# Moving averages of the pooled branch on GpSimd, and three changes in the order of ScalarE's small work, in a two-layer hybrid encoder

## The reference, cut to what matters

```python
h = rms_norm(x, norm_w)
proj = jnp.einsum('bld,dn->bln', h, w_in)
(aq, ak, av, ag, bq, bk, bv, bg, cq, ckv, ckr, cg, du, dg) = jnp.split(proj, split_points, axis=-1)
...
q = jnp.einsum('blr,rn->bln', rms_norm(cq_raw, q_lat_w), w_uq)      # branch c: the up-projections
kv = jnp.einsum('blr,rn->bln', rms_norm(ckv_raw, kv_lat_w), w_ukv)
...
# branch d: for group g of 128 channels, window w = 2, 4, 8, 16
mean = (jnp.take(csg, hi, axis=1) - jnp.take(csg, lo, axis=1)) / cnt   # moving mean of u over w tokens
outs.append(mean - u32[..., sl])
...
mixed = jnp.einsum('blgc,gcd->blgd', pooled, w_group).reshape(b, l, BRANCH_W) * scale
...
y = jnp.concatenate([ya * silu(ag), yb * silu(bg), yc * silu(cg), yd * silu(dg)], axis=-1)
return x + jnp.einsum('bln,nd->bld', y, w_out)
```

## Time and profile before

| what | value |
|---|---|
| time, median of 3 runs | 913.06 us (913.02 to 913.20) |
| the profiled execution's own time | 912.77 us |
| its span, first to last instruction | 911.0 us |
| PE, PEld, DVE, ACT, POOL busy | 899.7, 858.4, 637.0, 585.5, 0.2 us |
| granted clock of TensorE, mean | 1.00 |
| HBM read, written | 140.57, 2.10 MB |

### The profile page before, as it was taken

The page is one execution under the profiler, slowest core; times in us unless marked ns, Lnnn a source line. Parts: engine busy times, 40 slices in busy tenths (PEclk is TensorE's granted clock), DMA queues, the critical chain, the costliest instruction groups (busy, mean ns, idle before and its releaser), DMA issues.

```text
span 911.0 us, 18111 instructions
## 1 busy us (share of the span) xinstructions
PE 899.7 (99%) x7054; PEld 858.4 (94%) x7054; DVE 637.0 (70%) x1071; ACT 585.5 (64%) x1045; POOL 0.2 (0%) x4
## 2 busy tenths in 40 slices
PE   8999999999999999999999999999999999999998
PEld 7998998999999999999999989999999999999998
DVE  7785887768777776766665658876687667666552
ACT  7678756678666667745554588566686666675331
POOL 0000000000000000000000000000000000000000
PEclk9999999999999999999999999999999999999999
DMA  8654343343444343445455544334425344445562
GB/s 332 260 188 142 134 142 132 109 139 129 140 141 142 138 148 128 145 149 192 166 195 185 186 155 169 119 119 161 158 93 186 128 151 145 149 171 185 187 201 78
DMA packets 22997, 143.83 MB, mean 158 GB/s; under 512 B 2560, under 2 KB 4736, under 8 KB 6528
## 3 DMA queue, kind: packets, MB, share of 16 engines
q1 hardware_dynamic: 22768, 142.64, 44.0%
q10 hardware_dynamic: 144, 0.04, 0.0%
HBM read 140.57 MB, written 2.10 MB: 157 GB/s over the span
## 4 chain that ended last, share of the span: by engine, by line
PE 89%; ACT 7%; DVE 2%; issue 1%; DMA 1%; SPq 0%; ACTq 0%; DVEq 0%
PE dense L725 25%; PE dense L727 24%; PE dense L726 24%; PE s_ps L889 4%; PE o_ps L924 4%; ACT w_hi L1014 2%; PE norm_ps L845 2%; PE t_ps L905 2%; DVE w_lo L1319 1%; ACT qw L1087 1%; DMA x<-xt_dram 1%; PE swap_ps L860 0%; ACT sq L1084 0%; PE norm_ps L727 0%; PE swap_ps L727 0%
## 5 line engine op out<-in xcount | busy, mean ns | idle before, releaser
L725 PE MATMUL dense<-h_hi,w_hi 128*128 128x272 f32 (+2 forms) x1440 | 427.1, 297 | 1.5 <-DVE h_lo L1299 0.9
L727 PE MATMUL dense<-h_hi,w_lo 128*128 128x272 f32 (+2 forms) x1440 | 412.6, 287 | 0.0
L726 PE MATMUL dense<-h_lo,w_hi 128*128 128x272 f32 (+2 forms) x1440 | 410.6, 285 | 0.0
L1319 DVE TENSOR_TENSOR w_lo<-raw,w_hi 128x1024 fp32r<-128x1024 f32 (+1 forms) x257 | 313.3, 1219 | 88.4 <-ACT w_hi L1014 82.3
L1014 ACT ACTIVATE w_hi<-raw 128x1024 fp32r<-128x1024 f32 (+1 forms) x257 | 271.3, 1056 | 68.7 <-PE dense L727 53.9
L725 PEld LDWEIGHTS dense<-h_hi,w_hi 128*128 128x128 f32 x1440 | 271.3, 188 | 8.2 <-issue 3.8
L726 PEld LDWEIGHTS dense<-h_lo,w_hi 128*128 128x128 f32 x1440 | 271.5, 189 | 1.3
L727 PEld LDWEIGHTS dense<-h_hi,w_lo 128*128 128x128 f32 x1440 | 271.1, 188 | 0.0
L725 PE MATMUL dense<-y_hi,w_hi 128*128 128x272 f32 (+1 forms) x500 | 143.1, 286 | 2.3 <-ACT q_st L1059 1.3
L727 PE MATMUL dense<-y_hi,w_lo 128*128 128x272 f32 (+1 forms) x500 | 142.7, 285 | 0.0
L726 PE MATMUL dense<-y_lo,w_hi 128*128 128x272 f32 (+1 forms) x500 | 142.4, 285 | 0.0
(11 more groups left out here) (161 smaller groups left out, 813.4 us busy)
## 6 DMA issues: line engine op xcount, KB each, us to landing
raw<-w_stream_dram SPq DMA_DIRECT2D x128, 1024.0 KB, 4.8
out_dram<-x SPq DMA_DIRECT2D x8, 256.0 KB, 6.3
x<-xt_dram SPq DMA_DIRECT2D x3, 544.0 KB, 8.9
raw<-w_stream_dram SPq DMA_DIRECT2D x3, 512.0 KB, 7.5
con<-consts_dram SPq DMA_DIRECT2D x1, 984.0 KB, 7.4
x<-xt_dram SPq DMA_DIRECT2D x2, 272.0 KB, 4.8
raw<-w_stream_dram SPq DMA_DIRECT2D x2, 256.0 KB, 4.6
d_w<-consts_dram SPq DMA_DIRECT2D x2, 256.0 KB, 5.1
```

The lines of the kernel that those rows point to most:

```text
L725: nc.tensor.matmul(ps, whi, xhi, start=first, stop=False)
L726: nc.tensor.matmul(ps, whi, xlo, start=False, stop=False)
L727: return nc.tensor.matmul(ps, wlo, xhi, start=False, stop=last)
L1319: signal(nc.vector.tensor_tensor(w_lo[:, g % RING, 0:n], raw[:, e % RAW, CHUNK * half:CHUNK * half + n], w_hi[:, g % RING, 0:n].bitcast(F3 ...
```

## The change

It does five things.

1. `pool` leaves DVE and runs on POOL, in the order of the same plan, with buffers of its own (`slide`). The last instruction is split in two, a scaling and a subtraction. So per layer POOL runs 18 large instructions (10 adds, 4 scalings, 4 subtractions) and 8 with 8 columns; it begins a group as soon as its `du` row is rescaled, and waits for the preceding `mix` before the scaling.
2. `norm_ps` is free for PE's next sum when the logarithm has read it (new semaphore `norm_taken`), no longer when the exponential is done.
3. In ACT's table the inverse roots (`rope_fin`) move from 0.834 to 0.61 within a slot, that is from behind the `split` (0.71) to in front of it and right behind the `lift` (0.60). The squares (`rope_pre`) move from 0.11 to 0.62 of their slot, behind `p_out` and `s_exp`. For the heads of branch a and for `kr` the sum, its root and DVE's rotary stand one slot later, and the sub-norms (`sub_*`) avoid other slots than before.
4. ACT's `up_out` is planned tile by tile: in the first three chunks one tile is taken before a `split` and the other behind it, and in the last two all tiles are taken before it.
5. The `split` of chunk 18 of a layer moves up by 0.98 slot, and `kr`'s squares leave the up-projection.

```diff
+UP_TILES = (2, 2, 2, 4, 3)
...
 AT_TENSOR = dict(chunk=0.5, score=0.515, lat_stat=0.595, xsum=0.6, rope_stat=0.6, sub_stat=0.6, mix=0.605, pv=0.61,
                  p_turn=0.863, v_turn=1.817)
-AT_SCALAR = dict(rope_fin=-0.166, lat_fin=0.07, mix_out=0.09, lat_pre=0.097, sub_fin=0.1, rope_pre=0.11,
+AT_SCALAR = dict(rope_fin=-0.39, lat_fin=0.07, mix_out=0.09, lat_pre=0.097, sub_fin=0.1, rope_pre=0.62,
                  y_split=0.66, xscale=0.283, sub_pre=0.439, x_out=0.55, p_out=0.56, gate=0.65, s_exp=0.579,
-                 lift=0.6, up_out=0.705, split=0.71, x_square=0.72, y_gate=0.73, y_lat=0.72, lam_exp=0.793, v_out=1.297)
-AT_VECTOR = dict(sq_sum=0.2, rope_mid=0.25, s_max=-0.418, lam_dot=-0.35, sub_fin=-0.345, rope_fin=-0.34, lat_fin=0.055, head_out=0.17,
+                 lift=0.6, up_out=0.705, up_next=0.715, split=0.71, x_square=0.72, y_gate=0.73, y_lat=0.74, lam_exp=0.793, v_out=1.297)
+AT_VECTOR = dict(sq_sum=0.64, lat_sum=0.2, rope_mid=0.8, s_max=-0.418, lam_dot=-0.35, sub_fin=-0.345, rope_fin=-0.34, lat_fin=0.055, head_out=0.17,
                  y_split=0.75, pool=0.266, xscale=0.283, gate=0.7, s_scale=0.491, x_out=0.512, rescale=0.55,
                  x_add=0.614, split=0.71, lam_out=0.82, y_gate=0.76, y_lat=0.72)
 
 
-MOVED = {**{("lift", l, 3, 0): -0.55 for l in range(DEPTH)},
+MOVED = {**{("lift", l, 3, 0): -0.55 for l in range(DEPTH)}, **{("split", l, 18): -0.98 for l in range(DEPTH)},
...
+        kind = "lat_sum" if stage[:2] == ("sq_sum", "lat") else kind
...
                 if kind in ("aq", "ak"):
                     at(s, ("rope_pre", l, kind, i0 + j, j))
-                    at(s, ("rope_stat", l, kind, i0 + j))
-                    at(s + 1, ("rope_fin", l, kind, i0 + j))
+                    at(s + 1, ("rope_stat", l, kind, i0 + j))
+                    at(s + 2, ("rope_fin", l, kind, i0 + j))
...
-        at(s + 8, ("rope_pre", l, "kr", 0, None))
-        at(s + 9, ("rope_stat", l, "kr", 0))
-        at(s + 10, ("rope_fin", l, "kr", 0))
+        at(s + 9, ("rope_pre", l, "kr", 0, None))
+        at(s + 10, ("rope_stat", l, "kr", 0))
+        at(s + 11, ("rope_fin", l, "kr", 0))
 
         for c in range(U_CHUNKS):
-            at(s + 4 + c, ("up_out", l, c))
+            for j in range(UP_TILES[c]):
+                at(s + 4 + c, ("up_next" if c < 3 and j else "up_out", l, c, j))
...
         if kind in ("aq", "ak", "bq", "bk"):
-            taken |= {pair_slot(p) + 4, pair_slot(p) + 5}
+            taken |= {pair_slot(p) + 5, pair_slot(p) + 6}
...
+    slide = sb("slide", [128, 2, L + 16])
...
         def norm_free(*stage):
             n = norm_order[stage]
             if n:
-                pe.wait_ge(rn_ready, n)
+                pe.wait_ge(norm_taken, n)
...
-            link(nc.scalar.activation(rn[:, t0:L], norm_ps[:, t0:L], ACT.Ln, scale=1.0 / width, bias=eps_c[:, 0:1]))
+            signal(nc.scalar.activation(rn[:, t0:L], norm_ps[:, t0:L], ACT.Ln, scale=1.0 / width, bias=eps_c[:, 0:1]),
+                   norm_taken, n + 1)
             signal(nc.scalar.activation(out_, rn[:, t0:L], ACT.Exp, scale=-0.5), rn_ready, n + 1)
...
+        def pool(l, g, j):
+
+            u = row[:, j, :]
+            pa, pb = slide[:, 0, :], slide[:, 1, :]
+            wide = L + 16
+            gp.wait_ge(scaled, scaled_of(l, "du", g))
+            link(nc.gpsimd.tensor_tensor(pa[:, 1:wide], u[:, 0:wide - 1], u[:, 1:wide], ALU.add))
+            src, dst, lo, hi, step = pa, pb, 1, wide, 1
+            for _ in range(g):
+                link(nc.gpsimd.tensor_tensor(dst[:, lo + step:hi - step], src[:, lo:hi - 2 * step],
+                                             src[:, lo + 2 * step:hi], ALU.add))
+                lo, hi, step = lo + step, hi - step, 2 * step
+                src, dst = dst, src
+
+            edge = con[:, CC["edge"] + 16 * g:CC["edge"] + 16 * g + 16]
+            link(nc.gpsimd.tensor_tensor(src[:, 8:16], src[:, 8:16], edge[:, 0:8], ALU.mult))
+            link(nc.gpsimd.tensor_tensor(src[:, L:L + 8], src[:, L:L + 8], edge[:, 8:16], ALU.mult))
+            n = 4 * l + g
+            if n:
+                gp.wait_ge(mixed_ps, n)
+            link(nc.gpsimd.tensor_scalar(src[:, 8:8 + L], src[:, 8:8 + L], 1.0 / (2 << g), None, ALU.mult))
+            nc.gpsimd.tensor_tensor(pooled[:, :], src[:, 8:8 + L], u[:, 8:8 + L], ALU.subtract).then_inc(pooled_ready, 1)
+            gp.wait_ge(pooled_ready, n + 1)
+
+        gp.wait_ge(s_tab, 16)
+        for stage, *what in vector_plan:
+            if stage == "pool":
+                pool(*what)
```

More of the change, by code:

```diff
@@ L1040, in lift, with up_out @@
                    scaled_no[(l, p, j)])
-        def up_out(l, c):
-            for j in range(up_tiles(c)):
-                ps = wait_tile(act, l, "up", c, j)
-                q0 = first_query(l)
-                if c < 2:
-                    i, out_ = 2 * c + j, q_st[:, 2 * c + j, q0:L]
-                    free = (scores_ready, store_free(l, "c", "q", i))
-                elif c == 2:
-                    out_, free = c_st[:, 6 + j, q0:L], (scores_ready, store_free(l, "c", "q", j))
-                elif c == 3:
-                    out_, free = k_st[:, j, :], (scores_ready, store_free(l, "c", "k", j))
-                else:
-                    n = K_BLOCKS[j][1]
-                    out_, free = v_st[0:n, j, :], (pv_done, sums_before[store_free(l, "c", "v", 3)])
-                if free[1]:
-                    act.wait_ge(*free)
-                src = ps[0:K_BLOCKS[j][1], :] if c == 4 else ps[:, 0:L - q0] if c < 3 else ps[:, 0:L]
-                signal(nc.scalar.activation(out_, src, ACT.Copy), up_taken, UP_TILES * l + up_no(c, j))
+        def up_out(l, c, j):
+            ps = wait_tile(act, l, "up", c, j)
+            q0 = first_query(l)
+            if c < 2:
+                i, out_ = 2 * c + j, q_st[:, 2 * c + j, q0:L]
+                free = (scores_ready, store_free(l, "c", "q", i))
+            elif c == 2:
+                out_, free = c_st[:, 6 + j, q0:L], (scores_ready, store_free(l, "c", "q", j))
+            elif c == 3:
+                out_, free = k_st[:, j, :], (scores_ready, store_free(l, "c", "k", j))
+            else:
+                n = K_BLOCKS[j][1]
+                out_, free = v_st[0:n, j, :], (pv_done, sums_before[store_free(l, "c", "v", 3)])
+            if free[1]:
+                act.wait_ge(*free)
+            src = ps[0:K_BLOCKS[j][1], :] if c == 4 else ps[:, 0:L - q0] if c < 3 else ps[:, 0:L]
+            signal(nc.scalar.activation(out_, src, ACT.Copy), up_taken, sum(UP_TILES) * l + up_no(c, j))
         def buffers_free(*stage):
@@ L1505, in _, with link @@
                 run[stage](*what)
+    @block.gpsimd
+    def _(gp):
+        own = [0]
+        def link(ins):
+            own[0] += 1
+            ins.then_inc(gp_own, 1)
+            gp.wait_ge(gp_own, own[0])
+        def pool(l, g, j):
[23 more added lines that the diff above has]
+                pool(*what)
     ctx.close()
```

28 lines of the change are left out of this document (5 added, 23 removed).

## The result

The changed kernel takes 921.97 us (median of 4 runs, 920.21 to 922.5), the kernel before 913.04; the ratio is 1.0094 (95% interval 1.0077 to 1.0112). The forecast was 908.0 us, with a range up to 916. The sign was wrong, and the time lies outside the range.

The account below looks back on a forecast made before the run. PE, busy 99% of the span, was taken as the bound, so only its waits could change; the terms -4.4, -0.8, -1.5, -0.6, +1.5, +0.3, +0.4 summed to -5.1 us, giving 908.0 us, range 905 to 916.

Parts of the forecast that it names:

- new wait at `pv`: Around slot 38 and in layer 1, root, `sq`, `qw` and `split` ahead of `p_t` make PE wait: +1.5 us.
- Up-projection: In both layers, tiles lifted singly around the `split` end all six PE waits for ACT: -4.4 us.
- the 0.23 us added to each: Loss beyond the named idle time, added to each piece of PE's waiting for ACT.
- The freeing at the logarithm: Norm bank freed earlier saves 0.45 us of a wait no row shows, with PE the only waiter: counted as nothing.
- Squares behind `p_out`: Squares now stand behind `p_t`, ending PE's waits of 0.66 us at 777.25 and 0.40 us elsewhere: -1.5 us.
- the sum that waited for `qw`: PE's sum comes a chunk later and no longer waits for `qw`: -0.6 us.
- Roots behind lifts: At pair 5 of layer 1 the lift now stands ahead of the root, ending PE's 0.58 us wait: -0.8 us.
- small waits elsewhere: Roots wait in front of a `split` in some 20 slots, which may make `p_out` late: +0.4 us.
- Pooling on GpSimd: Group 3's `pooled` is in time for `mix` in layer 0, 0.6 us late in layer 1: +0.3 us counted.
- Rival A: POOL and DVE collide in SBUF, so PE waits 9.8 us before the last `mix` of both layers: 917.5 us; chance 0.18.
- Rival B: ACT's waits move instead of going, four or five further `p_t` or lifts late: 912 us, no change; chance 0.16.
- Both signs of being wrong: `mix` waits over 2 us a layer, or ACT's `p_t` and lifts hold PE up in more than five places.

Follow-up runs that it names:

- e10: Changed kernel with the averages back on VectorE and the roots back at -0.166; 909.95 us.
- e3: Kernel before with only the up-projection lifted singly, the `split` of chunk 18 earlier and `kr` a slot later; 911.2 us.
- e11: e5 with the norm bank free at the logarithm instead of after the root; 912.33 us.
- e5: Kernel before with squares, their halves, rotation's middle and sums later; root kept at -0.166 and norm bank freed by the root; 912.45 us.
- e4: The order's kernel: kernel before with the new places of sums, squares and roots and the bank free at the logarithm, without up-projection and GpSimd parts; 918.85 us.
- e14: e4 with the roots at -0.37 instead of -0.39, so behind the squares of their slot and ahead of the `split`; 913.47 us.
- e2: Kernel before with only the averages moved to GpSimd; 917.33 us.
- e12: Changed kernel with only the root moved back from -0.39 to -0.166; 914.06 us.
- e1: Changed kernel with only the averages put back on VectorE; 917.62 us.

## Why the prediction was wrong

The sum was -5.1 us; without the two losing parts the rest of the change gives -3.0 (e10). One term was also added up wrongly: the new wait at `pv`, 0.6 + 0.23 us in each of two layers, is 1.7 and not 1.5.

*Up-projection, -4.4.* Mechanism right: the six waits went. The size is 3.0 us, exactly their idle time; the 0.23 us added to each was not there. A mechanism was missing besides: 1.2 us were given back at the norm bank (e3). The freeing at the logarithm, which I had priced at 0, cures half of it (e10 against e11, 2.4 us).

*Squares behind `p_out`, -1.5, and the sum that waited for `qw`, -0.6.* In e5 the wait at 777 us and the one for `qw` went, in e11 0.3 of 1.1 us for `p_t` is left. 0.8 us of waits for `yt` came in their place, which I had not counted: -0.5 in all.

*Roots behind lifts, -0.8, and small waits elsewhere, +0.4.* **This is the first step that failed.** I saw that a root would wait in front of a `split` in some 20 slots, allowed 0.4 us for `p_out` that comes late by it, and stopped there. The root's place costs 6.5 us in the order's kernel and 7.9 in the changed one. What stood behind it in the queue and mattered most in the order's kernel was the next tile's squares (5.4 us, e14), the start of a chain that leads over DVE and PE to the next root. I had counted their move as a gain only. Nor was the root's move needed for the lift of pair 5, layer 1: PE waits for no lift in e11, with the root at -0.166, and for three in e4 (1.2 us). ACT's waits show the cost: ACT idles 24.1 us for the sums before, 46.2 in e4, 20.3 in e11. But idle time of ACT isn't what decides: e14 has 43.1 and takes only 1.1 us more than e11.

*A new wait at `pv`, +1.5.* It is there, at the step named: `p_t` 0.50 us at 155.0, start differences 1.23 less the 0.46 of a moved sum, 0.8 us; in layer 1 1.17 less 0.46, 0.7 us. It belongs to the root's place and is gone in e11 and e14.

*Pooling on GpSimd, +0.3.* **The second step that failed,** by its size: 4.1 to 4.35 us. The place was right (last `mix` of layer 1). A large instruction was taken at 0.9 us, and in the changed kernel it has 0.93. What was wrong are the small ones, 0.28 against 0.68 (2.7 us for four), the 0.08 us between two instructions, which I had left out (0.9 us), and so 13.8 us where I had 11.0 (the window was some 11 us in the changed kernel, 10.4 before). Alone the chain would take 0.67 + 1.47 + 0.20 + 0.20 + 0.89 + 0.76 = 4.2 us for group 2, and 0.74 more for group 3 with its third add, 9.1 us for both, and with the gaps 10.0: inside the window of 10.4. So without collisions it would have been in time. An add of 287 columns alone is 0.67 us against DVE's 0.46, a ratio of 1.5. The Trainium skill (GPSIMD Engine Reference, Performance versus the Vector engine) has 1.96 for an add of 2048 columns; no add here shows that ratio without a collision. Then comes the price of lateness: I had PE's loss equal to the delay, and 1.6 us of clock came on top in the profiled executions.

*Rival A* had the place and the cause, but not the size: 1.36 us a large instruction, where it is 0.93, and 9.8 us late in both layers; in e2 it is 2.8 in one. That its 917.5 us is near e2's 917.33 is luck. The Trainium skill's rule that I had set beside it (SBUF — State Buffer, Who interferes with whom) has the two engines exclude each other for an instruction's whole length. The rows agree: 8 columns took 1.06 us behind a `w_lo`, and `y_lo`, 0.76 us instead of 0.42, shows it in the other direction. My 0.18 for this rival was low; the tight window was in the trace, and so was DVE at 70%. *Rival B* had the right engine: ACT's waits moved. It gave 912 us, as it too saw only `p_t` and lifts. Both signs of being wrong that the text named were met: a wait of over 2 us at `mix` in layer 1 (2.76), and six places where ACT's `p_t` and lifts hold PE up (three each), where it allowed five.

Together: -3.0 (e10) + 4.1 (e12) + 7.9 (changed kernel against e12) = +9.0. This is a chain of differences and has to close; that the two costs hardly depend on each other is seen from the other way round, 7.7 for the root (e1 against e10) and 4.35 for the averages (e1).
